# The second mixer's output: feature blocks by head, turned between retention pieces; four product tiles side by side; keys between tiles; rows turned one by one

## The reference

```python
rq, rk, rv, rg, dq, dk, dv = split(rmsnorm(x, g) @ w_in)
ry = rmsnorm(retention(rq, rk, rv))                     # 4 heads of 128, per head
ret_out = silu(rg) * ry
dy = diff_attention(dq, dk, dv, lam)                    # 4 heads of 128
diff_out = rmsnorm(dy, diff_subln_g) * (1.0 - li)
x = x + concatenate([ret_out, diff_out], -1) @ w_out    # 1024 x 1024
x = x + peer(rmsnorm(x, norm_ffn_g), peer_wq, subkeys, u, v)
return rmsnorm(x, final_norm_g)
```

## Time and profile before

| | |
|---|---|
| median of 3 runs | 2415.29 us (2405.51 to 2416.55) |
| the profiled execution | 2421.08 us |
| its span, first to last instruction | 2419.3 us |
| mean granted TensorE clock | 0.982 |
| TensorE busy | 2340.7 us (97%) |
| VectorE, GpSimd, ScalarE busy | 1340.5, 1184.9, 914.6 us |

### The profile page before, as it was taken

How to read it: one execution, slowest core, us unless ns; L and a number is a source line. 1 busy time by engine, 2 the same in 40 slices (tenths; PEclk the granted TensorE clock), 3 DMA queues, 4 the chain that set the end, 5 groups by cost and what they waited for, 6 DMA issues and landing times.

```text
span 2419.3 us, 30051 instructions
## 1 busy us (share of the span) xinstructions
PE 2340.7 (97%) x11557; PEld 1169.7 (48%) x11557; DVE 1340.5 (55%) x2761; ACT 914.6 (38%) x1091; POOL 1184.9 (49%) x558
## 2 busy tenths in 40 slices
PE   8999999999999989999999999999999999999998
PEld 4447544444444465544566334444444444444443
DVE  2646646455424633899798444545555554545455
ACT  3232333333323443211598333333333334444432
POOL 1000346665642347510000566666666666888873
PEclk9988999999999999999999999999999999999999
DMA  6020238898962227924487675666666666867551
GB/s 214 13 92 1 105 111 249 243 260 235 258 189 72 70 105 196 252 106 157 187 325 307 246 244 182 193 191 191 193 191 192 192 179 162 224 186 195 145 132 44
DMA packets 403384, 425.05 MB, mean 176 GB/s; under 512 B 275770, under 2 KB 342590, under 8 KB 392004
## 3 DMA queue, kind: packets, MB, share of 16 engines
q1 hardware_dynamic: 396932, 411.93, 56.3%
q10 hardware_dynamic: 6336, 11.54, 1.3%
HBM read 283.97 MB, written 72.35 MB: 147 GB/s over the span
## 4 chain that ended last, share of the span: by engine, by line
PE 70%; POOL 13%; DVE 7%; ACT 4%; DMA 2%; issue 2%; SPq 2%; POOLq 0%; ACTq 0%; DVEq 0%
PE ps L1776 39%; PE ps L2032 14%; POOL u_split L932 4%; POOL split L924 3%; PE ps L2071 3%; POOL split L938 2%; ACT u_split L1343 2%; PE ps L1554 1%; PE ps L1863 1%; PE ps L1861 1%; DMA gate_matrix<-split 1%; PE ps L1552 1%; PE ps L2048 1%; PE ps L2049 1%; POOL ring L945 1%
## 5 line engine op out<-in xcount | busy, mean ns | idle before, releaser
L1776 PE MATMUL ps<-split,arena 128*128 128x512 bf16 x3984 | 873.8, 381 | 20.6 <-DVE x_sb L2754 10.8
L1776 PEld LDWEIGHTS ps<-split,arena 128*128 128x128 bf16 x3984 | 390.6, 98 | 498.6 <-issue 32.8
L2032 PE MATMUL ps<-arena 128*128 128x512 bf16 x1920 | 417.7, 379 | 0.0
L938 POOL TENSOR_TENSOR split<-ring,split 128x1024 bf16<-128x1024 f32 x140 | 305.8, 2195 | 110.4 <-ACT split L1356 110.4
L823 POOL TENSOR_TENSOR split<-ring,split 128x4096 bf16<-128x4096 f32 x26 | 207.2, 7969 | 214.4 <-ACT split L1155 212.1
L2032 PEld LDWEIGHTS ps<-arena 128*128 128x128 bf16 x1920 | 187.9, 98 | 226.5
L1776 PE MATMUL ps<-arena,split 128*128 128x512 bf16 x1344 | 296.2, 380 | 1.2 <-DVE arena L2495 1.0
L932 POOL TENSOR_TENSOR u_split<-ring,u_split 128x1024 bf16<-128x1024 f32 x80 | 167.8, 2130 | 172.5 <-ACT u_split L1343 172.5
L2748 DVE TENSOR_TENSOR ps<-ps,arena 128x512 f32<-128x512 f32 x84 | 58.5, 697 | 317.1 <-ACT ps L1409 316.9
L924 POOL TENSOR_TENSOR split<-ring,split 128x1024 bf16<-128x1024 f32 x44 | 92.3, 2133 | 258.1 <-ACT split L1353 258.1
L1356 ACT ACTIVATE split<-ring 128x1024 bf16<-128x1024 f32 x140 | 145.2, 1053 | 192.9 <-POOL ring L945 66.9
(11 more groups left out here) (357 smaller groups left out, 3109.3 us busy)
## 6 DMA issues: line engine op xcount, KB each, us to landing
ring<-in_peer_v SPq DMA_DIRECT2D x32, 2048.0 KB, 7.6
ring<-in_peer_u SPq DMA_DIRECT2D x20, 2048.0 KB, 11.8
ring<-in_w_ff SPq DMA_DIRECT2D x16, 2048.0 KB, 8.1
gate_matrix<-split SPq DMA_DIRECT2D x16, 2048.0 KB, 7.5
arena<-gate_matrix SPq DMA_DIRECT2D x32, 1024.0 KB, 6.1
arena<-in_peer_u SPq DMA_DIRECT2D x48, 512.0 KB, 4.8
turned_table<-u_split SPq DMA_DIRECT2D x48, 512.0 KB, 5.5
ring<-turned_table SPq DMA_DIRECT2D x12, 2048.0 KB, 8.9
```

The lines of the kernel that those rows point to most:

```text
L938: pool.tensor_tensor(part_place(i, 1), block, part_place(i, 0), ALU.subtract).then_inc(v_lo, 1)
L1776: mm = pe.matmul(dst, a(k), b(k), start=n == 0, stop=n == len(terms) - 1)
L2032: mm = pe.matmul(up_bank(j), a, b, start=n == 0, stop=n == len(terms) - 1)
```

## The change

Feature block k of y2 is now columns 128 k to 128 k + 127, one head: blocks 0 to 3 are retention heads, 4 to 7 attention heads. `w_out_2` is loaded with the matching rows, and the gain of each attention head is one column. The blocks are turned in the order 4, 5, 6, 7, 0, 1, 2, 3: two between the third head's update and the products behind it, the rest between product groups. The first four product tiles stand in four banks and take blocks as they come (`out2_products`); tiles 4 to 7 follow one by one with the subkeys' transposes between them. The peer transposes are made row by row for six blocks, row 0 ahead of tile 7, and blocks 6 and 7 inside the first query tile. VectorE, ScalarE and GpSimd have their orders changed to suit.

```diff
-        y2T_hi = part(arena, 10240, KD, T, dt=BF16)
-        y2T_lo = part(arena, 12288, KD, T, dt=BF16)
+        y2T = [[part(arena, at + 256 * half, T, dt=BF16) for at in (8192, 8704, 9216, 9728, 2048, 2560, 3072, 3584)] for half in range(2)]
+        Y2_BLOCKS = (4, 5, 6, 7, 0, 1, 2, 3)
+        Y2_BANKS = (6, 7, 6, 7, 6, 7, 4, 5)
+        norm_spare = part(arena, 12288, D)
...
+            if stage == "peer":
+                return (0, 1, 4, 5, 6, 7, 0, 1)[k]
...
                     for h in range(H):
-                        sp.dma_start(gains[64 + 16 * h:80 + 16 * h, G_Y2:G_Y2 + KD],
-                                      ins["diff_subln_g_2"][0].rearrange("(p k) -> p k", k=KD)).then_inc(small_in, 16)
+                        sp.dma_start(gains[:, G_Y2 + H + h:G_Y2 + H + h + 1],
+                                      ins["diff_subln_g_2"][0].rearrange("(p k) -> p k", k=1)).then_inc(small_in, 16)
...
-            w_out_2 = ins["w_out_2"][0].rearrange("(p k) n -> p k n", k=KD)
+            w_out_2 = ins["w_out_2"][0].rearrange("(k p) n -> p k n", k=KD)
...
             pre_late(SOON)
             split_low(27, 3)
+            for t in range(2):
+                inverse_rms(1, D, 69 + t, t)
             pre_late(SOON + 1)
-            for t in range(NT):
+            for t in range(2, NT):
                 inverse_rms(1, D, 69 + t, t)
             pre_late(SOON + 2)
...
-            for i in range(1, H):
-                decayed_keys(i)
-                in2_out(24 + i)
-                ret_squares(i - 1)
-            ret_squares(H - 1)
+            decayed_keys(1)
+            in2_out(25)
+            ret_squares(0)
+            decayed_keys(2)
+            in2_out(26)
+            ret_squares(1)
+            decayed_keys(3)
+            y2_high(0)
+            y2_high(1)
+            ret_squares(2)
+            in2_out(27)
+            ret_squares(3)
+            y2_high(2)
+            y2_high(3)
             split_high(26, 2, 7)
-            turned_high("out2", G_Y2, y2T_hi)
+            for n in range(4, KD):
+                y2_high(n)
             split_high(27, 3, 8)
-
+            keys_across(0)
+            keys_across(1)
             for t in range(NT):
                 act.wait_ge(mm_out, MM["wq"] - NT + t + 1)
-                sum_squares(x_sb[:, t, :], ps[:, 6:8, :].rearrange("p a b -> p (a b)"), t)
...
+                sum_squares(x_sb[:, t, :], norm_spare, t)
+                if t == 0:
+                    keys_across(2)
+                    keys_across(3)
             turned_high("peer", G_FFN2)
...
+            def row_turns(stage, src_k, rows_done, t):
+                pe.wait_ge(xn_done, rows_done + t + 1)
+                for k in range(6):
+                    mm = pe.transpose(bank(turn_bank(stage, k))[:, t * P:(t + 1) * P], src_k[:, t, :, k], ident)
...
+            def late_turn(stage, src_k, k):
+                pe.wait_ge(turned_lo, TURN_LO[stage] + k - 5)
+                turn(k, turn_bank(stage, k), lambda t: src_k[:, t, :, k])
...
                 for n, (a, b, k) in enumerate(terms):
+                    if late is not None and n in (3, 4):
+                        late_turn(turning, late, n + 3)
...
+            def turn_y2(first, last, ready):
+                pe.wait_ge(y2_ready, ready)
+                for n in range(first, last):
+                    if 2 <= n < 6:
+                        pe.wait_ge(turned_lo, TURN_LO["out2"] + n - 1)
+                    turn(Y2_BLOCKS[n], Y2_BANKS[n], lambda t: y2[:, t, Y2_BLOCKS[n] * P:(Y2_BLOCKS[n] + 1) * P])
...
                 ret_update(i)
+                if i == 2:
+                    turn_y2(0, 2, 2 * NT)
                 in2_matmuls(at + 14, 320 + 64 * i // 3)
             ret_value(H - 1)
...
+            def out2_products(tiles, blocks):
...
+                for n in tiles:
+                    rows_ = slice(n % 4 * P, (n % 4 + 1) * P)
+                    for b in blocks:
+                        k = Y2_BLOCKS[b]
+                        if n == 0:
+                            pe.wait_ge(turned_lo, TURN_LO["out2"] + b + 1)
+                        for i, (half, w) in enumerate(((0, wh), (0, wl), (1, wh))):
+                            mm = pe.matmul(out2_bank(n), y2T[half][k][:, rows_], w[:, k, :],
+                                           start=b == 0 and i == 0, stop=b == KD - 1 and i == 2)
...
+            turn_y2(2, 4, 4 * NT)
...
+            out2_products(range(4), (0, 1))
+            turn_y2(4, 7, 7 * NT)
+            out2_products(range(4), (2, 3))
+            turn_y2(7, 8, 8 * NT)
+            out2_products(range(4), (4, 5, 6))
+            out2_products(range(4), (7,))
...
+            out2_products((4,), range(KD))
+            pe.wait_ge(keys_in, 16)
+            turn_keys(0)
+            turn_keys(1)
+            pe.wait_ge(mm_out, MM["out2"] + 4)
+            out2_products((5,), range(KD))
+            turn_keys(2)
+            turn_keys(3)
+            pe.wait_ge(mm_out, MM["out2"] + 5)
+            out2_products((6,), range(KD))
             pe.wait_ge(keys_out, 4)
-            turn_features("peer", xn, 3 * NT, True)
+            row_turns("peer", xn_rows, 3 * NT, 0)
+            pe.wait_ge(mm_out, MM["out2"] + 6)
+            out2_products((7,), range(KD))
+            for t in range(1, NT):
+                row_turns("peer", xn_rows, 3 * NT, t)
...
             for i in range(1, H):
                 decayed_scores(i)
+                if i == 2:
+                    dif_rows((0, 1))
                 ret_rows(i - 1)
+                if i == 2:
+                    dif_rows((2, 3))
                 ret_states(i)
                 if i == 2:
...
+                    for t in range(3):
+                        gated_row(0, t)
+                if i == 3:
+                    y2_low(0)
+                    y2_low(1)
+                    for t in range(3):
+                        gated_row(1, t)
             ret_rows(H - 1)
...
+            for t in range(3):
+                gated_row(2, t)
+            for h in range(3):
+                gated_row(h, 3)
+            y2_low(2)
+            y2_low(3)
+            for t in range(NT):
+                gated_row(3, t)
+            for n in range(4, KD):
+                y2_low(n)
+            add_linear(MM["out2"], 23, (2, 3, 0, 1, 2, 3, 2, 3))
             turned_low("peer", G_FFN2)
```

More of the change, by code:

```diff
@@ L1271, in ret_squares, with y2_high, keys_across @@
                     sum_squares(y2[:, t, h * DV:(h + 1) * DV], spare_row, h * NT + t)
+            def y2_high(n):
+                k = Y2_BLOCKS[n]
+                act.wait_ge(turned, TURN["out2"] + n + 1)
+                act.activation(y2T[0][k], bank(Y2_BANKS[n]), ACT.Copy, scale=gains[:, G_Y2 + k:G_Y2 + k + 1]).then_inc(turned_hi, 1)
+            def keys_across(b):
+                act.wait_ge(keys_turned, b + 1)
+                act.activation(keysT[:, 4 * b:4 * b + 4, :], bank(4 + b % 2).rearrange("p (g n) -> p g n", g=4), ACT.Copy).then_inc(keys_out, 1)
             decayed_keys(0)
@@ L1957, in _, with out2_bank, turn_keys @@
                 ret_update(i)
+                if i == 2:
+                    turn_y2(0, 2, 2 * NT)
                 in2_matmuls(at + 14, 320 + 64 * i // 3)
             ret_value(H - 1)
-            pe.wait_ge(y2_ready, 2 * NT * H)
-            turn_features("out2", y2)
-            for c in range(2):
-                linear_chunk(S_OUT2 + c, MM["out2"] + 4 * c, False, y2T_hi, y2T_lo, None if c else "out2")
-            pe.wait_ge(keys_in, 16)
-            for b in range(4):
+            def out2_bank(n):
+                return bank((2, 3, 0, 1, 2, 3, 2, 3)[n])
+            def out2_products(tiles, blocks):
+                c = tiles[0] // 4
+                wh, wl = high((S_OUT2 + c) % 2, KD), low((S_OUT2 + c) % 2, KD)
+                for n in tiles:
[7 more added lines that the diff above has]
+                                           start=b == 0 and i == 0, stop=b == KD - 1 and i == 2)
+                    if blocks[-1] == KD - 1:
+                        mm.then_inc(mm_done, 1)
+            def turn_keys(b):
                 if b >= 2:
@@ L2477, in add_linear @@
                     dst = x_sb[:, t, c * CW:(c + 1) * CW]
-                    dve.tensor_tensor(dst, bank(2 + (done_before + n) % 2), dst, ALU.add).then_inc(mm_out, 1)
+                    dve.tensor_tensor(dst, bank(banks[n]), dst, ALU.add).then_inc(mm_out, 1)
                     if n >= 5:
@@ L2521, in _ @@
             ff_accumulate(6)
-            own.did(dve.tensor_scalar(gains[64:P, G_Y2:G_Y2 + KD], gains[64:P, G_Y2:G_Y2 + KD], 1.0 - LAMBDA_INIT, None, ALU.mult))
+            own.did(dve.tensor_scalar(gains[:, G_Y2 + H:G_Y2 + KD], gains[:, G_Y2 + H:G_Y2 + KD], 1.0 - LAMBDA_INIT, None, ALU.mult))
             own.wait()
@@ L2614, in _, with dif_rows, gated_row @@
                     ret_states(0)
+            def dif_rows(heads):
+                dve.wait_ge(rstd_done, 18)
+                for h in heads:
```

(22 more changed lines are left out.)

25 lines of the change are left out of this document (17 added, 8 removed).

## The result

| | before | after |
|---|---|---|
| median | 2418.65 us (20 runs, 2405.51 to 2423.94) | 2406.14 us (20 runs, 2396.05 to 2408.95) |
| the profiled execution, its span | 2421.08, 2419.3 us | 2407.53, 2405.5 us |
| mean granted clock | 0.982 | 0.985 |
| TensorE busy, matmul records | 2340.7 us, 11557 | 2321.9 us, 11355 |

The ratio is 0.995 [0.9939, 0.996]: 12.5 us less (9.7 to 14.8), faster by 0.5%. Forecast were 2403.4 out of a median of 2415.29, so 11.9 less. The profiled execution came out 13.6 shorter.

What follows compares the result with a forecast made beforehand. TensorE, busy 97%, was taken as the bound, losing 19.5 us (10.8 idle, 8.7 low clock) in one stage. Its stage 13.6 shorter, minus 1.7 for low clock, gave 11.9: median 2403.4 from 2415.3, range 2396 to 2413.

Steps and rivals of the forecast that it cites:

- The excess of 19.5, as 10.8 idle and 8.7 low clock: Second mixer to first query tile: 75.0 us against 55.5 of work at high clock; no gain beyond 19.5 possible.
- Rows of y2 by need: Turning y2 in groups needing 16, 28 and 32 rows: 6.25 gap and low clock behind it disappear, margin 1.7 us.
- four tiles side by side: Second mixer's first four product tiles: same 192 products, all ending together at 904.1, no wait for weights.
- keys between tiles: Key transposes between product tiles: 16 at 0.111 each, copies hidden behind 5.2 us tiles; idle 2.04 and 0.69 go.
- Row 0 ahead of tile 7: Added TensorE wait for row 0's root on GpSimd, behind table rows and a low half: 1.4 us, between 0 and 2.5.
- Rows 2 and 3: Late turned rows after tile 7: waits of 1.4 (row 2's root behind GpSimd's next pair) and 0.7 us.
- The end: High and low halves pace the first query tile; stage ends at 941.2, not 954.8: 13.6 less if clock stays high.
- The low clock in the tail, 1.7: Last 8 us of the stage: likely low-clock cost of 1.7 us, cutting the gain from 13.6 to 11.9.
- What costs nothing: Reordered second weight matrix, four small gain loads, inverse roots, ScalarE's square: taken as 0, loads 1.5 us at most.
- After the stage: TensorE unbroken to 1171, so later stages start earlier by the same amount; weight chunks 28 to 30 move along.
- The fourth case: Gain returns later, where gate matrix stores and expert rows are paced by transfers: 0 to 5 us gained; chance 0.10.
- The numbers: Whole kernel: 11.9 us off, profiled execution 2421.1 to 2409.2, median 2415.3 to 2403.4; 12.1 us tells from no change.

Runs made afterwards that it cites:

- the fillers: Kernel before plus 24 unread products or 48 unread transposes in TensorE's 6.25 us gap ahead of the y2 transposes: 2413.07 and 2413.74 us, ratios 0.9972 and 0.9979.
- fill_transposes: Kernel before plus 48 unread transposes in TensorE's 6.25 us gap ahead of the y2 transposes: 2413.74 us, ratio 0.9979, stage 89.75 us.
- the second profile: The changed kernel run and profiled once more, nothing altered: 2406.01 us, ratio 0.9936, stage 82.13 us.
- roots_late: Changed kernel with the inverse roots of rows 0 and 1 back behind GpSimd's second pair of table rows: 2410.71 us, ratio 0.9968, stage 90.82 us.
- neither half alone: Changed kernel with the PEER part undone, 2411.47 us, stage 88.24; kernel before with only the PEER part of the change, 2415.82 us, stage 92.47.
- peer_part_undone: The mixer's half alone: changed kernel with last four tiles, keys, turned features and roots ordered as before: 2411.47 us, ratio 0.9982, stage 88.24 us.

## Why the prediction came out right, point by point

**The excess of 19.5, as 10.8 idle and 8.7 low clock.** Right in kind, and the clock's part is too large: the fillers alone took 5.6 us out of the stage by the clock, with the other idle times left in or slightly longer (1.24 for 0.92). The 72 transposes that took 16.4 at the low level still take 10.5 with the clock at 1.00 (fill_transposes), and not 8.0, since the low halves pace them.

**Rows of y2 by need, four tiles side by side, keys between tiles.** Right. The last retention product was forecast to end at 880.7 and ended at 880.4; no wait for the rows; the clock at 1.00 from 880 to 932; tiles 0 to 3 through at about 904 (ScalarE's next weight split begins at 903.84; forecast 904.1). The 6.25, 0.93, 2.04 and 0.69 are gone.

**Row 0 ahead of tile 7.** The wait of 1.4 (0 to 2.5) was 0, and 0.66 in the second profile: inside the range, at its lower end. The term that was off is the landing of the table rows. They were taken to arrive 10.5 to 12 behind the low half of chunk 26; they came 9.4 behind it (895.57 to 904.93). From the issue at 896.06 to the landing were 8.9, where before had 11.5. That one microsecond of landing is one of TensorE is borne out by the two profiles (0.61 later, 0.66 of wait), and for the root behind it by roots_late, which adds the clock to it.

**Rows 2 and 3.** Forecast were waits of 1.4 and 0.7; measured 2.34 and 0.60. The mechanism was right for the change as made: row 2's root stands behind the pair (928.49), and the row follows it at once, at 0.75. What the prediction lacked is that the row too is held by GpSimd's copy or low half, so that an earlier root alone gains nothing. TensorE was also at row 2 earlier than forecast (927.8 and not 929.5), so that 0.9 of the 1.4 that did not come ahead of row 0 was paid here.

**The end.** Row 3's turns at 931.6 (forecast 932.3) and the first query tile at 940.85 (941.2). Stage 13.7 shorter, against 13.6 ahead of the clock term.

**The low clock in the tail, 1.7.** This is the term that was mis-sized. The clock did fall there (932 to 935), but it cost 0.2 to 0.25: the turns and products of the tail are paced by the high and low halves, and a slower TensorE is hidden behind them. The estimate took the price from 16 transposes in one block, as 3.47 less 16 by 0.11. But such a block takes 2.63 to 2.69 with the clock at 1.00 (fill_transposes), so even there no more than some 0.8 was the clock. Without the term the forecast is 13.6, and the profiled execution shows 13.55. So close a hit is partly luck: the stretch behind the stage can differ by some microseconds, and the missing wait for row 0 and the longer one for row 2 cancel in part.

**What costs nothing.** The small loads of the gains, taken as 0 with 1.5 us at most, show no cost in the two profiles: TensorE comes to the stage at 859.24 where it came at 859.50. No run shows the 1.5.

**After the stage.** Right: the rest is 1464.65 for 1464.5 in the two profiles. The fourth case, a gain of 0 to 5 because the rest comes back later, is outside the interval of the medians (9.7 to 14.8).

**The numbers.** The stage says 13.7, the medians 12.5 (9.7 to 14.8), and the forecast was 11.9: the medians can't tell these apart. They also hold how often an execution escapes the low stretch at 167, about 10 us each time; 2405.51, 2410.08 and 2410.76 among the twenty of before are probably such ones. The median of before moved from 2415.29 to 2418.65 between three runs and twenty, so the forecast of 2403.4 is met by its difference and not by its sum. The prediction laid 0.64 on 9 to 15 us and left open on which side of 12.1 it would fall; the median's 12.5 doesn't decide that either.

**Left open.** What decides whether the clock falls behind the 1.40 at 167 in an execution. Why filling the first gap kept the clock up 45 us later. And 3.8 of the 13.7 belongs to neither half alone; its cause is read from the rows of peer_part_undone and not tried by a kernel of its own.

## What to carry to other kernels

Look for TensorE's idle time and for what the clock does behind it: unread work in a gap of 6.25 us won 5.6 of the stage without any new order, and in one of 1.40 us in the attention nearly as much as the whole change. When a piece of an order is moved up, follow what it waits for through every engine; the mixer's half alone ran into roots that stood behind a load, and gave a third of its gain back. Where a wait is put down to a VectorE row, look at what GpSimd runs in the same microseconds before moving the producer.

## What the runs showed of the hardware that was not expected

- Transposes held the high clock as products did: 48 of them in 5.40 us, and the turns behind them at 2.07 for 16 in place of 3.68.
- A wait can cost more than itself, or nothing by the clock. The 6.75 us ahead of row 0 cost 9.2, since the turns and a whole product tile behind it ran low (6.89 for 5.34). The low stretch behind the waits of 2.34 and 0.60 in the tail cost 0.2 to 0.25, since other engines paced the work there.
- A VectorE row of 1024 columns took 0.75 alone, 1.50 when it began with GpSimd's 1.04 copy, and 2.06 when it began 0.6 into GpSimd's 2.13 low half. GpSimd's one-column operation of 0.19 took 0.75 beside a VectorE row.
- Executions of one kernel differ by 10 us, and the profiles of other kernels and the mean clocks put that down to one stretch of low clock, 30 us long, behind a gap of 1.40 us. With 2.78 us of transposes there all six executions were of the short kind, with a mean granted clock of 0.992 to 0.994; the profiled one had no low stretch there.
